# Two layers of experts on one core: how the residual is added, the order of the work behind the last expert, and the layout of the scan stage's inputs

## What is computed

```python
# first block, layer i = 0, 1
mixed = rglru_mixer(h, ...) if i == 0 else shortconv_mixer(h, ...)
h = layer_norm(ALPHA * h + mixed, ln_g[i, 0], ln_b[i, 0])
ffn = hierarchical_moe(h, ...)     # 32 experts, two for each token
h = layer_norm(ALPHA * h + ffn, ln_g[i, 1], ln_b[i, 1])     # "ffn0", "ffn1"
# the meta tokens are dropped behind layer 1

# the expert part
hb = silu(xb @ w_gate[e]) * (xb @ w_up[e])
y += gate * (hb @ w_down[e])

# second block: a state-space mixer (s5), a feed-forward part, latent attention, a feed-forward part
```

## Time and profile before

| | |
|---|---|
| median of 3 executions | 1953.24 us (1948.21 to 1956.41) |
| the profiled execution | 1956.41 us, span 1954.6 us |
| TensorE busy | 1625.2 us, 83% |
| VectorE busy | 532.3 us, 27% |
| ScalarE busy | 212.8 us, 11% |
| GpSimd busy | 75.7 us, 4% |
| DMA | 540.07 MB, 276 GB/s over the span |
| granted TensorE clock, mean | 0.913 of full speed |

### The profile page before, as it was taken

How to read it: one execution, slowest core, us unless ns; L and a number is a source line. 1 busy time by engine, 2 the same in 40 slices (tenths; PEclk the granted TensorE clock), 3 DMA queues, 4 the chain that set the end, 5 groups by cost and what they waited for, 6 DMA issues and landing times. The chain is left out here.

```text
span 1954.6 us, 28797 instructions
## 1 busy us (share of the span) xinstructions
PE 1625.2 (83%) x12983; PEld 1078.3 (55%) x12983; DVE 532.3 (27%) x1271; ACT 212.8 (11%) x487; POOL 75.7 (4%) x97
## 2 busy tenths in 40 slices
PE   7999668888766999755646646799999998999998
PEld 6655445564444876433323333686886446578643
DVE  5652234432134214204211111621210023421002
ACT  2311011001100001000200000120110003211000
POOL 2001000000000100000000000330000010000000
PEclk9999889889887999978878787899999999899999
DMA  9357999999998645999999999534443425043410
GB/s 339 143 205 319 379 422 418 420 421 422 419 420 339 245 197 226 420 418 414 418 424 414 412 422 388 220 136 177 162 170 132 145 92 187 29 165 137 172 43 21
DMA packets 104440, 540.07 MB, mean 276 GB/s; under 512 B 7326, under 2 KB 9438, under 8 KB 86908
## 3 DMA queue, kind: packets, MB, share of 16 engines
q1 hardware_dynamic: 102428, 531.24, 68.1%
q0 software_dynamic: 1888, 6.95, 1.1%
HBM read 531.89 MB, written 6.29 MB: 275 GB/s over the span
## 5 line engine op out<-in xcount | busy, mean ns | idle before, releaser
L717 PE MATMUL ps<-ring,work 128*32 128x256 f32 x3968 | 292.5, 460 | 230.8 <-DMA ring<-in_moe_w_up 229.4
L717 PEld LDWEIGHTS ps<-ring,work 128*32 128x32 f32 x3968 | 160.9, 132 | 355.4 <-issue 309.8
L694 PE MATMUL ps<-ring,work 128*128 128x512 f32 x768 | 331.0, 592 | 0.0
L668 PE MATMUL ps<-hT,ring 128*128 128x256 f32 (+2 forms) x1488 | 329.7, 384 | 0.0
L668 PEld LDWEIGHTS ps<-hT,ring 128*128 128x128 f32 x1488 | 283.0, 191 | 45.3 <-issue 3.3
L694 PEld LDWEIGHTS ps<-ring,work 128*128 128x128 f32 x768 | 145.7, 190 | 182.2 <-issue 181.3
L729 PE MATMUL ps<-ring,multi 128*32 128x256 f32 x1984 | 125.2, 395 | 17.4 <-ACT multi L1422 12.1
L1987 DVE TENSOR_TENSOR rowb<-rowb,ps 128x128 f32<-128x128 f32 x64 | 18.3, 287 | 373.9 <-ACT rowb L1417 373.9
L1993 DVE COPY multi<-ps 128x256 f32<-128x256 f32 x64 | 27.1, 424 | 286.1 <-PE ps L729 286.1
L737 PE MATMUL ps<-rowb,hres 128*128 128x128 f32 (+1 forms) x640 | 103.6, 302 | 0.2 <-DVE rowb L1652 0.2
L737 PEld LDWEIGHTS ps<-rowb,hres 128*128 128x128 f32 (+1 forms) x640 | 85.5, 196 | 17.1 <-issue 1.8
(11 more groups left out here) (437 smaller groups left out, 1267.7 us busy)
## 6 DMA issues: line engine op xcount, KB each, us to landing
ring<-in_moe_w_gate SPq DMA_DIRECT2D x62, 2048.0 KB, 19.2
ring<-in_moe_w_up SPq DMA_DIRECT2D x62, 2048.0 KB, 23.7
ring<-in_moe_w_down SPq DMA_DIRECT2D x62, 2048.0 KB, 21.6
ring<-in_w_ff SPq DMA_DIRECT2D x32, 2048.0 KB, 8.2
ring<-in_sc_w_in SPq DMA_DIRECT2D x6, 2048.0 KB, 17.8
ring<-in_lru_w_in SPq DMA_DIRECT2D x4, 2048.0 KB, 15.8
ring<-in_ssm_w_glu SPq DMA_DIRECT2D x4, 2048.0 KB, 18.8
ring<-in_lru_w_out SPq DMA_DIRECT2D x2, 2048.0 KB, 20.0
```

What stands on the lines that cost most here:

```text
L668: mm = pe.matmul(ps[:, bank, 0:n], w[:, k, P * c:P * c + P], hT[:, k, t0:t0 + n], start=(k == 0), stop=(k == DC - 1))
L694: mm = pe.matmul(ps[0:m, 2 + 2 * b + hf, :], left[:, kk, t0:t0 + m], w[:, k, 512 * hf:512 * hf + 512], start=(kk == 0), stop=(kk == 4 * la ...
L717: mm = pe.matmul(ps[32 * q:32 * q + 32, bank, 0:256].rearrange("p (u n) -> p u n", u=2), x[:, k, :], gu[:, k, :, P * q:P * q + P], start=( ...
```

## The change

1. The residual is added by TensorE. At experts 4 and 5 (`KEEP_AT`), behind `weigh_in`, four matmuls by block with ALPHA times the identity (`alphas`, made by VectorE at expert 1 in a free part of `hT`) add the residual to the sums. The four L2051 by block go, and VectorE's statistics and its subtraction read the sums in PSUM.
2. `value_load` of TensorE moves from behind the last expert to expert 1. `keep_busy(10)` goes in layer 0 and becomes `keep_busy(1)` in layer 1.
3. Of the meta tokens only the last two are normalised behind the experts of layer 0 (`NTAIL`). Block one's normalisation doesn't stand behind the meta sum any more; the matmul of the meta squares stands behind the transposes of block one, and ScalarE's root for the meta tokens behind its copies of block one. The last four meta operations stand inside block two's statistics.
4. A new semaphore `ffn{l}_taken` is raised when VectorE has read the sums; `sc_first` and `s5_inputs` wait for the second of these instead of `ffn{l}_var`.
5. In layer 1, ScalarE writes `hT` in the order (token within the chunk, chunk), so that `s5_inputs` reads neighbours.

```diff
+KEEP_AT = (4, 5)
+        alphas = hT[:, 0, 0:P]
+        NTAIL = CONV_B - 1
@@ TensorE, experts
+                def keep_rows(b):
+                    for q in range(4):
+                        pe.matmul(ps[:, q, SEQ * (b - 1):SEQ * b].rearrange("t (p k) -> t k p", k=DC), alphas,
+                                  hres[:, b, :].rearrange("t (k p) -> t k p", k=DC)[:, :, 32 * q:32 * q + 32],
+                                  start=False, stop=False, skip_group_check=True)
@@
                     if e == 1:
                         pe.wait_ge(*nth(f"spread_out{l}", 1))
                         pe.wait_ge(*nth(f"rounds_known{l}", 1))
+                        rounds = pe.value_load(rounds_i[0:1, l:l + 1], min_val=1, max_val=MAX_ROUNDS)
                     if e >= 1:
                         weigh_in(e - 1)
+                    if e in KEEP_AT:
+                        keep_rows(KEEP_AT.index(e) + 1)
@@
                 weigh_in(NE - 1)
-                rounds = pe.value_load(rounds_i[0:1, l:l + 1], min_val=1, max_val=MAX_ROUNDS)
@@
                 pe.end_ifs()
-                keep_busy(10)
+                if l == 1:
+                    keep_busy(1)
@@ TensorE, behind moe(0)
-            for name in ("meta_sum", "meta_square"):
-                pe.wait_ge(*nth(name, 1))
-                pe.matmul(ps[:, 4 if name == "meta_sum" else 5, 0:NMETA], ones[:, :], meta_acc[:, 0 if name == "meta_sum" else 1, :],
-                          start=True, stop=True).then_inc(S("meta_summed" if name == "meta_sum" else "meta_squared"), 1)
+            pe.wait_ge(*nth("meta_sum", 1))
+            pe.matmul(ps[:, 4, 0:NTAIL], ones[:, :], meta_acc[:, 0, :], start=True, stop=True).then_inc(S("meta_summed"), 1)
             def sc_first(i):
                 transposes("ffn0", [1, 2], "ffn0_normed", bank=6, only=i)
+                if i == 0:
+                    pe.wait_ge(*nth("meta_square", 1))
+                    pe.matmul(ps[:, 5, 0:NTAIL], ones[:, :], meta_acc[:, 1, :], start=True, stop=True).then_inc(S("meta_squared"), 1)
@@ TensorE, s5_inputs
-                                       chunked[r, k, :, 32 * i:32 * i + 32], start=(k == 0), stop=(k == CHUNK - 1),
+                                       hT[r, :, NMETA + NCH * k + 32 * i:NMETA + NCH * k + 32 * i + 32], start=(k == 0), stop=(k == CHUNK - 1),
@@ ScalarE, evac_turned
+                        if n == "ffn1":
+                            A(hT[:, 4 * h:4 * h + 4, NMETA:T].rearrange("p m (k c) -> p m k c", k=CHUNK)[:, :, :, 32 * i:32 * i + 32],
+                              ps[:, bank + j % 2, :].rearrange("p (m c k) -> p m k c", m=4, k=CHUNK), ACT.Copy).then_inc(S(f"{n}_hT"), 1)
+                            continue
@@ ScalarE, behind the experts
                 deviations(f"ffn{l}", only=0)
+                evac_turned(f"ffn{l}", blocks[-2:], bank=6, only=0)
                 if l == 0:
                     act.wait_ge(*nth("meta_squared", 1))
-                    A(meta_acc[:, 2, :], ps[:, 5, 0:NMETA], ACT.Sqrt, ...)
-                evac_turned(f"ffn{l}", blocks[-2:], bank=6, only=0)
+                    A(meta_acc[:, 2, :], ps[:, 5, 0:NTAIL], ACT.Sqrt, ...)
                 deviations(f"ffn{l}", only=1)
@@ VectorE, expert 1
+                    if e == 1:
+                        link(V.tensor_scalar(alphas, ident[:, :], ALPHA, None, ALU.mult))
@@ VectorE, behind the experts
                 for i, b in enumerate((1, 2)):
-                    x = tmps[i % 2]
-                    for q in range(4):
-                        ins = V.scalar_tensor_tensor(out=x[...], in0=unpacked(hres[:, b, :])[...], scalar=ALPHA,
-                                                     in1=ps[:, q, SEQ * i:SEQ * i + SEQ]..., op0=ALU.mult, op1=ALU.add)
-                    link(ins)
-                    statistics(f"ffn{l}", i, b)
+                    x, sums = tmps[i % 2], ps[:, 0:4, SEQ * i:SEQ * i + SEQ]
+                    V.bn_stats(stats[:, i, 0:6], sums[:, 0:2])
+                    if l == 0 and i == 1:
+                        dve.wait_ge(*nth("meta_sd", 1))
+                        ...                              # reciprocal, three products and sums, meta_normed
+                    link(V.bn_stats(stats[:, i, 6:12], sums[:, 2:4]))
+                    V.bn_aggr(mean_var[:, i, 0:2], stats[:, i, :]).then_inc(S(f"ffn{l}_var"), 1)
+                    ...
+                    V.scalar_tensor_tensor(out=x..., in0=sums, scalar=mean_var[:, i, 0:1],
+                                           in1=gain_bc..., op0=ALU.subtract, op1=ALU.mult).then_inc(S(f"ffn{l}_taken"), 1)
+                    dve.wait_ge(*nth(f"ffn{l}_taken", i + 1))
+                    dve.wait_ge(*nth(f"ffn{l}_sd", i + 1))
+                    link(V.reciprocal(mean_var[:, i, 3:4], mean_var[:, i, 2:3]))
+                    V.scalar_tensor_tensor(out=hres[:, b, :], in0=x, scalar=mean_var[:, i, 3:4], in1=bias_bc,
+                                           op0=ALU.mult, op1=ALU.add).then_inc(S(f"ffn{l}_normed"), 1)
                     if l == 0 and i == 0:
                         dve.wait_ge(*nth("meta_summed", 1))
                         ...                              # mean, difference, square, meta_square, now 2 columns wide
-                    normalised(f"ffn{l}", i, b, plain)
```

More of the change, by code:

```diff
@@ L122, in first_and_second_block @@
         share("left_ready", [("lru_z", 8), ("sc_z", 8), ("s5_y", 8), ("glu_done", 8), ("oT", 8)])
+        share("meta_by_dve", [("meta_sum", 1), ("meta_square", 1), ("meta_normed", 1)])
+        share("taken", [("ffn0_taken", 2), ("ffn1_taken", 2)])
         share("gated", [("lru_conv", 8), ("sc_gated", 8), ("s5_rotated", DC)])
@@ L1027, in sc_first @@
                     if i == 0 and kind == "bg":
-                        pe.wait_ge(*nth("ffn0_var", 2))
+                        pe.wait_ge(*nth("ffn0_taken", 2))
                     if i == 0:
@@ L1118, in _ @@
                 if i == 0:
-                    pe.wait_ge(*nth("ffn1_var", 2))
+                    pe.wait_ge(*nth("ffn1_taken", 2))
                 s5_inputs(i)
@@ L2048, in moe @@
                 for i, b in enumerate((1, 2)):
-                    x = tmps[i % 2]
-                    for q in range(4):
-                        ins = V.scalar_tensor_tensor(out=x[:, 256 * q:256 * q + 256].rearrange("t (p k) -> t p k", k=DC),
-                                                     in0=unpacked(hres[:, b, :])[:, 32 * q:32 * q + 32, :], scalar=ALPHA,
-                                                     in1=ps[:, q, SEQ * i:SEQ * i + SEQ].rearrange("t (p k) -> t p k", k=DC),
-                                                     op0=ALU.mult, op1=ALU.add)
@@ L2055, in moe @@
-                    link(ins)
-                    statistics(f"ffn{l}", i, b)
+                    x, sums = tmps[i % 2], ps[:, 0:4, SEQ * i:SEQ * i + SEQ]
+                    V.bn_stats(stats[:, i, 0:6], sums[:, 0:2])
+                    if l == 0 and i == 1:
+                        dve.wait_ge(*nth("meta_sd", 1))
+                        link(V.reciprocal(meta_acc[:, 2, :], meta_acc[:, 2, :]))
+                        link(V.tensor_tensor(meta_d, meta_d, over_d(meta_acc[:, 2, :]), ALU.mult))
+                        link(V.tensor_tensor(meta_d, meta_d, par[:, :, 12].unsqueeze(2).to_broadcast([P, DC, NTAIL]), ALU.mult))
+                        V.tensor_tensor(hT[:, :, NMETA - NTAIL:NMETA], meta_d, par[:, :, 13].unsqueeze(2).to_broadcast([P, DC, NTAIL]), ALU.add)\
+                            .then_inc(S("meta_normed"), 1)
@@ new lines, in moe @@
+                    link(V.bn_stats(stats[:, i, 6:12], sums[:, 2:4]))
+                    V.bn_aggr(mean_var[:, i, 0:2], stats[:, i, :]).then_inc(S(f"ffn{l}_var"), 1)
+                    if i == 0:
+                        dve.wait_ge(*nth("rows_ready", 2 * (ln_order.index(f"ffn{l}") + 1)))
+                    dve.wait_ge(*nth(f"ffn{l}_var", i + 1))
+                    V.scalar_tensor_tensor(out=x.rearrange("t (q n) -> t q n", q=4), in0=sums, scalar=mean_var[:, i, 0:1],
+                                           in1=gain_bc.rearrange("t (q n) -> t q n", q=4),
+                                           op0=ALU.subtract, op1=ALU.mult).then_inc(S(f"ffn{l}_taken"), 1)
@@ L2059, in moe @@
                         dve.wait_ge(*nth("meta_summed", 1))
-                        link(V.tensor_scalar(meta_acc[:, 3, :], ps[:, 4, 0:NMETA], 1.0 / D, None, ALU.mult))
-                        link(V.tensor_tensor(meta_d, meta_x, wide16(meta_acc[:, 3, :]), ALU.subtract))
+                        link(V.tensor_scalar(meta_acc[:, 3, :], ps[:, 4, 0:NTAIL], 1.0 / D, None, ALU.mult))
+                        link(V.tensor_tensor(meta_d, meta_x, over_d(meta_acc[:, 3, :]), ALU.subtract))
                         link(V.tensor_tensor(meta_x, meta_d, meta_d, ALU.mult))
@@ L2063, in moe @@
                         V.tensor_reduce(meta_acc[:, 1, :], meta_x.rearrange("p c t -> p t c"), AX.X, ALU.add).then_inc(S("meta_square"), 1)
```

(8 more changed lines are left out.)

18 lines of the change are left out of this document (9 added, 9 removed).

## The result

The changed kernel takes 1931.01 us (median of 4 runs, 1928.86 to 1939.25), the kernel before 1952.17 us beside it (4 runs, 1948.21 to 1956.41). The ratio is 0.9902, 95% interval 0.9878 to 0.9925: 1% faster. The profiled execution took 1932.28 us (span 1930.5 us), against 1956.41 (1954.6) before.

The account below looks back on a forecast made before the run. Bound taken: weight transfers inside expert stages, then a serial normalise-turn-start piece after each layer's last expert. Savings 9.8 + 8.5 = 18.3 us from the 1953.2 us median give 1935 us, range 1929 to 1942.

Parts of the forecast that it names:

- Layer 0, 9.8 us: End of layer 0's experts: first product of the short-convolution stage at 623.6 instead of 633.37, saving 9.8 us.
- Layer 1, 8.5 us: End of layer 1's experts: L1075, where the scan stage begins, at 1241.4 instead of 1249.82, saving 8.5 us.
- The idle piece: TensorE's issue wait at layer 1's branch, held as before: free of the branch at 1229.15, transposes at 1229.9.
- the two L1062 groups: Layer 1's spreading products, now reading neighbours: 3.0 and 2.6 us instead of 3.90 both times.
- from the end of the first group to the second: Layer 1, between the spreading groups: transposes at 1235.5, second L1062 after 1.8 to 2.65 us, taken as 2.4.
- `keep_rows`, 2.6 us each, hidden: Experts 4 and 5, both layers: residual matmuls of 2.6 us each, about 10 in all, under the wait for weights.
- The weights: Layer 0's next stage: first three sc_w_in landed at about 626, needed at 623.6, 626 and 628.5.
- Register load, 0 (bounds to 5.5): Moving TensorE's register load from before the branch saves 0 us; 0 to 1.3, or 5.5 if the whole piece.
- Rival 3: The register load, not the branch, is the 5.5 us issue piece: 1931 to 1932 us; chance 0.10.
- Rival 1: Without fills TensorE's clock is lower in layer 0's first products and layer 1: saving 13.2, 1940 us; chance 0.15.
- Rival 2: Second expert stage ends with the weight stream and gives back layer 0's saving: only 8.5 us, 1945; chance 0.10.
- Rival 4: Short-convolution projections never return to 2.4 GHz without fills: up to 72 us more, about 2007 us; chance 0.03.

Follow-up runs that it names:

- the two kernels with eight fills: Changed kernel with skips moved by satisfied waits and keep_busy(8) in both layers: padding of 161 entries, 1933.63 us; 161 and 208, 1929.71 us.
- the padded kernel: Changed kernel with 182 more instructions, satisfied semaphore waits, in TensorE's list in layer 0's experts: 1928.44 us, ratio 0.9885 to the kernel before.

## Why the prediction was right, and where it was off

- **Layer 0, 9.8 us: measured 9.84.** The place of the late thing was right as well: the branch out of the block, not VectorE. Fills 6.6 us of it, the order of the meta rows 2.5, the residual 1.6 (each measured by a kernel of its own, so they overlap and don't add up exactly).
- **Layer 1, 8.5 us: measured 9.57.** Three terms of the sum were mis-sized. The idle piece was 4.88 us, not 6.03: the changed list has its branch at another place, and I had held that piece fixed. The transposes so start 5.94 us behind VectorE's first operation, not 6.7. And the two L1062 groups took 3.79 and 2.01 us where 3.0 and 2.6 were taken: together 5.8 against 5.6, so the mean was right though neither was. And from the end of the first group to the second, where 2.4 us were taken, it was 1.77, because the second transposes took 1.09 us.
- **`keep_rows`, 2.6 us each, hidden:** 1.99 us each, hidden in fact; 1.8 on the path when uncovered. The rule by which a strided output to PSUM should have been near the upper bound of 3.9 (the Trainium skill, "Advanced Engine Details and Errata", Memory Cachelines) is not borne out: eight products of 256 columns with a stride of eight took 1.95 to 1.99 us.
- **The weights** were thought to be there with time to spare, the third at 626. In that execution it landed at 627.71, and in the changed kernel at 630.45, 1.15 us before its first use at 631.60. The term was right by a small margin, and the two kernels with eight fills ran into it.
- **Register load, 0 (bounds to 5.5):** 0 to 0.6; the load itself lasts 0.49 and 0.32 us in the trace of before. Rival 3, that it is the whole piece, is refuted twice: the piece was 5.5 and 4.9 us after the change with the load gone, and it vanished by moving or shortening the jump with the load left alone.
- **Rival 1, the clock as the new cost,** came true in part: 1.8 us in the first spreading group, and 7.34 instead of 5.60 us in layer 0's first products as against fills. But the earlier trace rows of before has 7.42 there, with fills, so that was no new cost. The 5.1 us that the rival asked for (18.3 less 13.2) were not there.
- **Rival 2, the gain given back in the second expert stage:** not so; had it all been given back, that middle piece would have grown to 599.7 us, and it is 588.63, and at most 594.4 in any experiment. It varies too much from profile to profile to exclude a few us. **Rival 4:** the stretch of projections stays at full clock (1.00 from 634 to 712 us, TensorE busy for 77.26 of the 78); the slow stretch that I did meet was in the profile of before and elsewhere.
- **The remaining 4 us** between 1935 and 1931: 1.1 from layer 1, and the rest, 2.9 us, I can't tell from scatter. The start of the edited piece of layer 0 moved between 609.9 and 618.0 us from profile to profile, and the middle piece between 587.1 and 594.4.

That the number came out owes something to chance: the idle piece was treated as a fixed cost of the branch, while it depends on where the list is cut into pieces of 256, and the first experiment, with only fills removed, showed it at 0 in layer 1. Had the changed list fallen so, layer 1 would have saved about 0.8 us more, as in the padded kernel; VectorE is next in line and hides the rest.

## What to carry to other kernels

An idle piece ascribed to issue just behind a taken branch is not a property of the branch: look where it and its target lie in the engine's instruction list, and how long the jump is, before you budget it. Fill work that keeps the clock up is worth its price only when it ends before the data is there; here 7 to 8 us of fills bought back 1.7 and 1.8 us, and where the fills were short enough, the next wait (weights, accumulators) took the gain. And judge an edit of a few microseconds by the stretch from one event to the next, not by whole times, which here moved by 10 us with nothing changed (1928.86 to 1939.25 for the changed kernel).

## What the hardware did that I had not expected

- Jumping over 303 to 343 entries of TensorE's list cost 0 to 6.03 us by position alone, and in one kernel 5.21 us came three matmul instructions after the jump. What it waits for is one packet of 16,384 bytes, 256 entries: about 1 us of transfer (1226.68 to 1227.57), but some 6.3 us from the start of the branch to its end (6.28 and 6.33 before). The DMA engines are full there (share 1.00 and 418 GB/s in the changed kernel's row of that place); whether it is shorter with the DMA engines free was not tried. Two kernels were stopped in straight code too, for 2.78 and 1.25 us.
- With a stride of four in the moving operand 32 products took 3.99 us at 1.2 GHz and 3.90 at 2.4, with neighbours 3.79 and 2.01. A stride of eight in the output cost nothing that shows.
- TensorE's clock fell to 1.2 GHz for about 16 us of attention scores with TensorE busy throughout, in one of the thirteen profiled executions, and that cost 6.1 us (29.62 against 23.52). What set it off is open.
